# Two gaps in the on-chip memory: the weights start at multiples of 2048 bytes, the activations 128 bytes behind such multiples, and the constants lie last

## The reference

```python
def swiglu(x, w_up, w_down):
    gate, up = jnp.split(x @ w_up, 2, axis=-1)
    return (jax.nn.silu(gate) * up) @ w_down

def hybrid_mixer(h, w_in, rel_bias, w_branch_a, w_branch_b, w_out, pos):
    proj = h @ w_in                      # queries, keys, values of 20 heads, two gates
    ...                                  # 12 heads: dilated windows, 8 heads: neighbourhood
    merged = gate_a * (ya @ w_branch_a) + gate_b * (yb @ w_branch_b)
    return merged @ w_out

def reference(x, ffn1_norm, ffn1_w_up, ffn1_w_down, mix_norm, w_in, na_rel_bias, w_branch_a,
              w_branch_b, w_out, ffn2_norm, ffn2_w_up, ffn2_w_down, final_norm):
    pos = jnp.arange(x.shape[1])
    for l in range(DEPTH):
        x = x + 0.5 * swiglu(rms_norm(x, ffn1_norm[l]), ffn1_w_up[l], ffn1_w_down[l])
        x = x + hybrid_mixer(rms_norm(x, mix_norm[l]), w_in[l], na_rel_bias[l], w_branch_a[l],
                             w_branch_b[l], w_out[l], pos)
        x = x + 0.5 * swiglu(rms_norm(x, ffn2_norm[l]), ffn2_w_up[l], ffn2_w_down[l])
    return rms_norm(x, final_norm)
```

## Time and profile before

| | |
|---|---|
| median of 3 runs | 1189.58 us (1189.21 to 1190.63) |
| the profiled execution, its own time | 1189.71 us |
| its span, first to last instruction | 1187.9 us |
| PE busy | 1172.8 us, 99% of the span |
| LDWEIGHTS busy | 963.8 us, 81% |
| DVE busy | 717.1 us, 60% |
| ACT busy | 560.8 us, 47% |
| granted PE clock | 0.998 of full speed |
| bytes moved by transfers | 211.47 MB, 178 GB/s on average |

### The profile page before, as it was taken

The page is one execution under the profiler, slowest core; times in us unless marked ns, Lnnn a source line. Parts: engine busy times, 40 slices in busy tenths (PEclk is TensorE's granted clock), DMA queues, the critical chain, the costliest instruction groups (busy, mean ns, idle before and its releaser), DMA issues.

```text
span 1187.9 us, 15620 instructions
## 1 busy us (share of the span) xinstructions
PE 1172.8 (99%) x5632; PEld 963.8 (81%) x5632; DVE 717.1 (60%) x992; ACT 560.8 (47%) x767; POOL 59.3 (5%) x70
## 2 busy tenths in 40 slices
PE   8999999999999999999999999999999999999997
PEld 5888888888888888888888888878888888888885
DVE  5565557755766665555675555577557566655555
ACT  6444345555534544444464444465554445444342
POOL 3300003000200000000000000200002000000000
PEclk9999999999999999999999999999999999999999
DMA  9966564653433465556545555655443435655541
GB/s 279 278 212 207 177 222 163 200 175 111 139 140 144 157 212 184 190 177 207 182 166 188 188 185 192 230 177 177 142 142 108 164 137 177 214 192 196 179 174 36
DMA packets 145594, 211.47 MB, mean 178 GB/s; under 512 B 7648, under 2 KB 112272, under 8 KB 145296
## 3 DMA queue, kind: packets, MB, share of 16 engines
q1 hardware_dynamic: 142960, 206.33, 52.0%
q0 software_dynamic: 1920, 3.20, 1.2%
q10 hardware_dynamic: 672, 1.37, 0.4%
HBM read 209.77 MB, written 4.19 MB: 180 GB/s over the span
## 4 chain that ended last, share of the span: by engine, by line
PE 90%; DVE 4%; ACT 3%; issue 2%; DMA 1%; SPq 0%; POOLq 0%; POOL 0%; DVEq 0%; ACTq 0%
PE bank L1015 28%; PE bank L1017 27%; PE bank L1016 27%; PE bank L1198 2%; PE bank L1101 2%; PE bank L1171 2%; DVE w_lo L719 1%; PE bank L1183 1%; ACT w_hi L520 1%; ACT a_hi L528 1%; DVE a_lo L743 1%; PE bank L1161 1%; ACT probs L538 1%; DMA x<-x_dram 1%; DVE qk_raw L922 0%
## 5 line engine op out<-in xcount | busy, mean ns | idle before, releaser
L719 DVE TENSOR_TENSOR w_lo<-raw,w_hi 128x2048 fp32r<-128x2048 f32 x190 | 439.8, 2317 | 243.8 <-ACT w_hi L520 243.8
L520 ACT ACTIVATE w_hi<-raw 128x2048 fp32r<-128x2048 f32 x190 | 363.5, 1917 | 254.9 <-PE bank L1017 238.6
L1015 PE MATMUL bank<-w_hi,a_hi 128*128 128x512 f32 (+1 forms) x1152 | 460.8, 400 | 1.5 <-DVE probsT L801 0.4
L1017 PE MATMUL bank<-w_hi,a_lo 128*128 128x512 f32 (+1 forms) x1152 | 446.7, 388 | 0.0
L1016 PE MATMUL bank<-w_lo,a_hi 128*128 128x512 f32 (+1 forms) x1152 | 445.7, 387 | 0.0
L1015 PEld LDWEIGHTS bank<-w_hi,a_hi 128*128 128x128 f32 x1152 | 216.6, 188 | 49.7 <-issue 5.8
L1017 PEld LDWEIGHTS bank<-w_hi,a_lo 128*128 128x128 f32 x1152 | 216.4, 188 | 45.8
L1016 PEld LDWEIGHTS bank<-w_lo,a_hi 128*128 128x128 f32 x1152 | 217.0, 188 | 39.0
L1015 PE MATMUL bank<-w_hi,hT_hi 128*128 128x512 f32 x352 | 138.2, 393 | 0.5 <-DVE hT_lo L808 0.5
L1017 PE MATMUL bank<-w_hi,hT_lo 128*128 128x512 f32 x352 | 137.1, 390 | 0.0
L1016 PE MATMUL bank<-w_lo,hT_hi 128*128 128x512 f32 x352 | 137.0, 389 | 0.0
(11 more groups left out here) (89 smaller groups left out, 650.0 us busy)
## 6 DMA issues: line engine op xcount, KB each, us to landing
raw<-ffn_w_up_dram SPq DMA_DIRECT2D x172, 512.0 KB, 4.6
raw<-w_in_dram SPq DMA_DIRECT2D x92, 512.0 KB, 4.5
raw<-ffn_w_down_dram SPq DMA_DIRECT2D x88, 512.0 KB, 3.9
raw<-w_out_dram SPq DMA_DIRECT2D x16, 512.0 KB, 3.7
raw<-w_branch_b_dram SPq DMA_DIRECT2D x8, 512.0 KB, 3.6
bias_rows<-na_rel_bias_dram POOLq DMA_DIRECT2D x24, 128.0 KB, 5.9
bias<-bias_rows SPq DMA_DIRECT2D x2, 1536.0 KB, 8.7
raw<-ffn_w_up_dram SPq DMA_DIRECT2D x8, 256.0 KB, 6.4
```

Of the source, the lines that this page charges most:

```text
L520: act.activation(w_hi[slot][:, :], raw[slot][:, :], ACT.Copy).then_inc(hi_done, 1)
L719: dve.tensor_tensor(w_lo[slot][:, :], raw[slot][:, :], w_hi[slot][:, :].bitcast(F32), ALU.subtract).then_inc(lo_done, 1)
L1015: pe.matmul(dst, s_hi, m_hi, start=start, stop=False)
L1017: return pe.matmul(dst, s_lo, m_hi, start=False, stop=stop)
```

## The change

Two unused tensors are put into the memory, and the constants are moved from the middle towards the end. No instruction is added, removed or moved on any engine: apart from line numbers, the order of the instructions, their operands and their waits on all five engines are those of before. Only addresses differ.

```diff
+GAP = 1920
 ...
+        sb("gap", [P, GAP // 4])
         raw = [sb(f"raw{i}", [P, UNIT]) for i in range(RING)]
         w_hi = [sb(f"w_hi{i}", [P, UNIT], F32R) for i in range(RING)]
         w_lo = [sb(f"w_lo{i}", [P, UNIT], F32R) for i in range(RING)]
 
         x = sb("x", [P, TT, D])
         gain = sb("gain", [P, D])
 
+        sb("gap_activations", [P, 128 // 4])
         a_hi = sb("a_hi", [P, KT, SEQ], F32R)
         a_lo = sb("a_lo", [P, KT, SEQ], F32R)
 ...
         bias = sb("bias", [P, NA_HEADS, BIAS_ROWS, GRID_W])
-        cst = sb("cst", [P, C_ALL])
         hT_hi = sb("hT_hi", [P, 2, SEQ], F32R)
 ...
         credits = sb("credits", [P, 2 * RING])
+        cst = sb("cst", [P, C_ALL])
         warm = sb("warm", [P, NB], BF16)
```

## The result

The changed kernel takes **1209.19 us** (median of 4 runs, 1208.74 to 1209.89), the kernel before in the same session 1189.88 us. The ratio is 1.0164, with a 95% interval of 1.0151 to 1.0177. It is slower by 19.3 us, where no change was forecast and the range ended at 1193.

The account below looks back on a forecast made before the run. PE was taken as the bound, the time being product matmuls times pitch. Every term was 0 except 0.3 us allowed for the start: 1189.6 + 0 = 1189.6 us, likeliest 1189.5, 8-in-10 range 1137 to 1193.

Parts of the forecast that it names:

- What bounds the kernel: PE, busy 99%: 4560 product matmuls at 226.7 ns and 96 at 120 ns, 1045 us of a 1187.9 us span.
- The weights move from 128 to 0: I take 0: Moving operands of the products: crossing a multiple of 2048 costs nothing; start untested; 0, bounds -53 to +37 us.
- The distance between the two operands: I take 0 for the ninth to twelfth: Product matmuls: eight stationary-to-moving distances had one pitch, so new odd multiples of 128 cost 0; bounds -53 to +37 us.
- Other readers: ACT and DVE access memory beside PE without changing its pitch; main reason for 0 in the weights and distance terms.
- Identity, transposes, the slow products behind them, the conversions: Moved constants and buffers: 0 taken; transposes at most 2.1 us either way, slow products some 3 us unchanged, conversions hidden under PE.
- The start: Transfers until the last part of `x` lands, 6.44 us on the chain: 5% either way is 0.3 us.
- The gain in full: All product matmuls: fixed 13.3 ns come from operand starts and shrink to bf16's 2 ns; 1137 to 1140 us, chance 0.20.
- The small gain: Only disturbed pitches around transposes, transposes and start gain: 1184 us; a gain in part, 1140 to 1187, had 0.10.
- The slower rival: Every product matmul: the stream passes over the block being loaded, 128 bytes behind; some 4 ns each, 1208 us, chance 0.16.
- The checks I named: If right, after trace: 18 product pitches in 4.08 us, 256-column products at 120 ns, a loop chunk some 16.8 us.
- If the pitch for `hT_hi` and `a_hi` differ, it is the distance: Sign in the after trace: unequal pitches for these two stationary tensors would point to the distance between operands.
- The last sentence of the prediction: It called itself wrong if a matmul's fixed part depends on an address that the before trace never varied.

Follow-up runs that it names:

- e1: Changed kernel without the 128-byte gap before the activations, so weights and stationary blocks both at 0 modulo 2048: 1188.95 us, ratio to before 0.9991.
- e2: Changed kernel without the 1920-byte gap, so weights at 128 as before and stationary tensors at 256 modulo 2048: 1209.63 us, ratio 1.0167.
- e7: Matmul-only kernel, layers left out: 40 distances in steps of 4 and 8 bytes, fewer columns, bf16; fp32r 512-wide never below 226.67 ns, bf16 215.8 ns.
- e4: Matmul-only kernel, layers left out: table of pitches for 81 operand address pairs; 226.7 ns at distance 0, 232.4 ns at 128.
- e5: Changed kernel with weights at 128 modulo 2048 and stationary tensors 64 bytes behind them modulo 256: 1211.45 us, ratio 1.0177.
- e9: Matmul-only kernel, layers left out, alternating address pairs: 230.0 ns with only a matmul's own operand distance at 128, 228.6 with only the overlapped stream's.

## Why the prediction was wrong, point by point

**What bounds the kernel** held: the time is the number of product matmuls times their pitch, and 4212 pitches grew by 5.0 ns. The 512-wide and 256-wide counts, and the reading of pitches from starts, held as well.

**"The weights move from 128 to 0: I take 0"** held. e1 has the weights at 0 and the time of before. The argument from the 256-wide slices, that crossing a multiple of 2048 costs nothing, was right.

**"The distance between the two operands: I take 0 for the ninth to twelfth"** is the step that failed. The eight distances with one pitch were all multiples of 256, and the table shows that 256 is just the period: they were one distance seen eight times. The change put all of them to 128, and that costs 5.0 ns a matmul. I had written that odd multiples of 128 are not shown in the trace, gave the step bounds of -53 to +37 us, and then let the range end at 1193. The bound that no row excluded should have stayed in the range. The error was to count sightings without asking what they have in common.

**"Other readers"** held in its observation and failed as an argument. ACT and DVE beside PE do change nothing, and the table has the same pitches with both at rest. But I took that as a reason that no address matters. The conflict, if it is one, is between PE's own two operands.

**Identity, transposes, the slow products behind them, the conversions**: 94.1 to 93.3 us for transposes and attention, and 1.2 us gained from another kind to product, so the 0 was off by no more than the 2 us that I had allowed for the transposes. **The start**: `x` landed 0.4 us earlier, a little more than the 0.3 us that I had allowed for it.

**The gain in full** falls. At least the fixed 13.3 ns are there at every pair of addresses that was tried, and only bf16 is without them. The likeness that I gave it, 32 columns before a crossing and 128 bytes of offset, meant nothing. **The small gain** falls too.

**The slower rival** came near in size, 1208 us against 1209.2. It took its 4 ns from the disturbed pitches behind transposes, and the changed kernel has a like pattern all the time; but nothing in the rows set this price, so that it came so near to the 5.0 ns is in part luck. It had the place too: the distance of 128. Its mechanism, that the stream passes over the block's lines, is not shown: at distance 256 or 512 it passes over them just so, for nothing.

**The checks I named**: 18 pitches took 4.18 us and not 4.08; the 256-wide ones 118.7 and not 120 ns; a chunk of the loop 17.20 us (mean of 36) and not 16.81. "If the pitch for `hT_hi` and `a_hi` differ, it is the distance" could not speak, since the change puts both at one distance; only changing one group of addresses at a time, in e1 and e2, could. The last sentence of the prediction, on an address that the trace never varied, is what happened.

**The rule of two independent read ports** ("TensorE: Matmul & The Clock Gate", "Step-by-step: what each phase is for", in the Trainium skill) says that loading the next block takes no read bandwidth from the running matmul. I had read it as saying that no address matters, and for fp32r the table contradicts that: 226.7 against 232.4 ns with nothing changed but the distance, and the measurement decides. For bf16, 215.8 ns at three distances, the runs agree with it. The same page of the Trainium skill, section "Back-to-back issue gap", has N/2.4 + 2.5 ns, from which I estimate 215.8 ns for 512 columns. That is just what the bf16 lines of e7 show; for fp32r no pair of addresses comes closer to it than 226.7. The section calls this the gap of an isolated matmul and gives some 131 ns at 512 columns for a stream in which each matmul has its LDWEIGHTS; no run here shows that, the bf16 lines, which are such a stream, included.

**What stays open** is what happens inside the chip. Shown is that distance, and starts off multiples of 32, set the pitch. That a disturbed order of reads settles into step at distance 0 and never does at 128 is suggested by the patterns in e4 (314, 224, 231, 235, 229, 232 and then 227, 227, 226 at distance 256, which is 0; 228, 230, 232, 241, 233, 231 again and again at 128), but it was not tested. Nor was fp32 in its plain form with wide slices.

## What to carry to other kernels

Where a kernel is bound by back-to-back fp32r matmuls with slices of 384 or 512 columns, print the start addresses of both operands, and keep stationary minus moving at a multiple of 256 bytes, with the starts at multiples of 32; an unused tensor of 64 bytes between the two cost 1.8% here (e5). Compare pitches between the starts of matmuls, since busy share, idle time and clock look the same at 227 and 233 ns. And when a trace shows many values of something with one result, ask which remainder they share before taking the next value to be like them.

## What the runs showed of the hardware that I had not expected

- The pitch of 512-wide fp32r matmuls depends on the distance between the operands modulo 256 bytes: 226.7 ns at 0, 228.9 at 192, 232.4 at 128, up to 236.7 among starts in steps of 16 and 237.8 with both starts at 4. PE is busy 99% in the kernels of before and after alike, at a mean granted clock of 0.998.
- Both the block that is loaded under a running stream and the matmul's own block seem to count: 228.4 and 230.0 ns with one at 128, 233.4 with both (with the reservation made at e9).
- Fewer stationary columns never bring less than 226.7 ns (at distance 0, 231.7 for 32 and 226.7 for 128; at 128, 230.5 for 32 and 226.7 for 96), and the effect is not one of size alone: a 256-wide slice is faster at distance 128 (118.7 ns) than at 0 (120.0), a 384-wide one slower (176.1, 173.3).
- At the start of e4 and e9, where PE had been idle for 45 us and had then done four transposes, the pitch is 426 to 428 ns, the 512 columns at 1.2 GHz, at distance 0 and at 128 alike: at that level neither the fixed 13.3 ns nor the address shows. The profile's row for the clock reads 1.00 in this stretch (the figure before the last two), so it does not tell the two levels apart here. Windows and timeline of e4; at 226.7 ns the five would take 1.30 us:

```profile
46.00:48.50 2.50, 2.50 (x7) 1.96 (x7) 0.00 (x0) 0.00 (x0) 1.00 0.00 0
46.40 2.33 PE L66 MATMUL bank<-area 128*128 128x512 f32 x5
```
